# Stick-breaking attention: order of the score blocks and value products between two head pairs

## The reference, cut to what matters

```python
z = einsum('bhtd,bhsd->bhts', q, k) / sqrt(64)
log_1mb = where(s < t, log_sigmoid(-z), 0)
suffix = cumsum(log_1mb, axis=3, reverse=True) - log_1mb
a = exp(where(s < t, log_sigmoid(z) + suffix, -inf))
out = einsum('bhts,bhsd->bhtd', a, v)
```

## Time and profile before

| | |
|---|---|
| median of 3 runs | 1989.14 us (1988.02 to 1990.04) |
| span of the profiled execution | 1987.1 us |
| its own time with what lies around the span | not given |
| PE busy | 1948.0 us, 98% |
| DVE busy | 1116.1 us, 56% |
| ACT busy | 859.2 us, 43% |
| mean granted clock of PE | 0.997 |
| stage of the attention pairs | about 1031 to 1234 us of the span |

### The profile page before, as it was taken

How to read it: one execution, slowest core, us unless ns; L and a number is a source line. 1 busy time by engine, 2 the same in 40 slices (tenths; PEclk the granted TensorE clock), 3 DMA queues, 4 the chain that set the end, 5 groups by cost and what they waited for, 6 DMA issues and landing times.

```text
span 1987.1 us, 25948 instructions
## 1 busy us (share of the span) xinstructions
PE 1948.0 (98%) x10434; PEld 1588.1 (80%) x10434; DVE 1116.1 (56%) x1824; ACT 859.2 (43%) x1528; POOL 89.6 (5%) x109
## 2 busy tenths in 40 slices
PE   8999999999999999999999999999999999999997
PEld 6688877888888888888877778888898788888886
DVE  5677745644465444423648888884645465444323
ACT  4355642533343222222447777774435453222221
POOL 0100000000020000000200000011200020000000
PEclk9999999999999999999999999999999999999999
DMA  7111121333323333333322222113243223333331
GB/s 278 61 54 43 54 70 59 90 96 93 104 75 96 95 96 92 92 88 91 94 75 58 63 64 63 45 55 105 64 132 103 85 77 94 95 96 93 87 98 62
DMA packets 49432, 170.56 MB, mean 86 GB/s; under 512 B 5520, under 2 KB 8080, under 8 KB 48928
## 3 DMA queue, kind: packets, MB, share of 16 engines
q1 hardware_dynamic: 48816, 166.73, 27.9%
q0 software_dynamic: 496, 2.16, 0.3%
HBM read 166.77 MB, written 2.10 MB: 85 GB/s over the span
## 4 chain that ended last, share of the span: by engine, by line
PE 91%; DVE 6%; ACT 2%; issue 1%; DMA 0%; SPq 0%; DVEq 0%
PE acc L1852 56%; PE bank L1852 18%; PE acc L2006 2%; PE bank L1941 2%; PE bank L2188 1%; PE acc L2388 1%; PE bank L1978 1%; PE bank L2223 1%; PE bank L2126 1%; DVE bank L1216 1%; DVE w_lo L1136 1%; PE bank L2375 1%; PE bank L2409 1%; DVE residual L1222 1%; PE bank L1874 1%
## 5 line engine op out<-in xcount | busy, mean ns | idle before, releaser
L1136 DVE TENSOR_TENSOR w_lo<-w_raw,w_hi 128x1024 fp32r<-128x1024 f32 (+2 forms) x306 | 365.7, 1198 | 330.5 <-ACT w_hi L602 330.1
L1852 PE MATMUL acc<-act_hi,w_hi 128*128 128x512 f32 (+1 forms) x1096 | 431.0, 393 | 17.4 <-DVE w_lo L1136 9.6
L1852 PE MATMUL acc<-act_lo,w_hi 128*128 128x512 f32 (+1 forms) x1096 | 419.3, 383 | 0.0
L1852 PE MATMUL acc<-act_hi,w_lo 128*128 128x512 f32 (+1 forms) x1096 | 419.3, 383 | 0.0
L602 ACT ACTIVATE w_hi<-w_raw 128x1024 fp32r<-128x1024 f32 (+2 forms) x306 | 314.3, 1028 | 210.9 <-PE acc L1852 181.0
L1852 PEld LDWEIGHTS acc<-act_hi,w_hi 128*128 128x128 f32 x1096 | 206.4, 188 | 68.4 <-issue 16.1
L1852 PEld LDWEIGHTS acc<-act_hi,w_lo 128*128 128x128 f32 x1096 | 206.4, 188 | 44.1
L1852 PEld LDWEIGHTS acc<-act_lo,w_hi 128*128 128x128 f32 x1096 | 206.6, 188 | 43.2 <-issue 2.2
L1852 PE MATMUL bank<-act_hi,w_hi 128*128 128x512 f32 (+1 forms) x520 | 192.6, 370 | 1.2 <-DVE w_lo L1136 1.2
L1852 PE MATMUL bank<-act_lo,w_hi 128*128 128x512 f32 (+1 forms) x520 | 191.0, 367 | 0.0
L1852 PE MATMUL bank<-act_hi,w_lo 128*128 128x512 f32 (+1 forms) x520 | 190.9, 367 | 0.0
(11 more groups left out here) (457 smaller groups left out, 3182.7 us busy)
## 6 DMA issues: line engine op xcount, KB each, us to landing
w_raw<-w_all SPq DMA_DIRECT2D x282, 512.0 KB, 3.5
w_raw<-w_all SPq DMA_DIRECT2D x16, 384.0 KB, 3.3
residual<-xT SPq DMA_DIRECT2D x8, 256.0 KB, 7.7
cmp_w_k<-w1k SPq DMA_DIRECT2D x1, 2048.0 KB, 8.6
cmp_w_v<-w1v SPq DMA_DIRECT2D x1, 2048.0 KB, 12.7
w_raw<-w_all SPq DMA_DIRECT2D x8, 256.0 KB, 2.7
out_t<-residual SPq DMA_DIRECT2D x16, 128.0 KB, 1.7
ret_decay<-decay POOLq DMA_DIRECT2D x4, 256.0 KB, 3.3
```

The lines of the kernel that those rows point to most:

```text
L1136: TT(WL[:, c % RAW_RING, 0:nb * P], WR[:, c % RAW_RING, 0:nb * P], WH[:, c % HI_RING, 0:nb * P].bitcast(F32), ALU.subtract).then_inc(s_lo, 1)
L1852: ins = MM(bank[:, cols], w[:, at, k * P:(k + 1) * P], x, start=first and r == 0 and k == 0, stop=last and r == 2 and k == nb - 1)
```

## The change

The next pair's scores become one run, in the order of blocks 0, 1, first half of 4, first part of 3, first part of 2, second part of 3, second half of 4, second part of 2. It stands in front of all the values of the pair, behind all five copies of the transposed weights. The first two steps (6 matmuls) of the turn's first gemm are put ahead of the run, the other six follow the values. Two semaphores count the scores, one for blocks 0, first half of 4 and 2, the other for 1, 3 and second half of 4; ACT's Abs waits for these. In the last pair, which has no next one, the values too now wait for all copies. DVE's program is unchanged.

```diff
+BEFORE_SCORES = 2
...
             def sb_abs(p, b):
-                act.wait_ge(sem("sb_scored"), p * 5 + b + 1)
+                if b in (1, 3):
+                    act.wait_ge(sem("sb_scored_second"), 3 * p + (1 if b == 1 else 2))
+                else:
+                    act.wait_ge(sem("sb_scored_first"), 3 * p + {0: 1, 4: 2, 2: 3}[b])
+                if b == 4:
+                    act.wait_ge(sem("sb_scored_second"), 3 * p + 3)
...
+            def scores(p):
+
+                first, second = sem("sb_scored_first"), sem("sb_scored_second")
+                scored(0, parts_of(0), p).then_inc(first, 1)
+                scored(1, parts_of(1), p).then_inc(second, 1)
+                scored(4, parts_of(4)[0:1], p).then_inc(first, 1)
+                scored(3, parts_of(3)[0:1], p)
+                scored(2, parts_of(2)[0:1], p)
+                scored(3, parts_of(3)[1:2], p).then_inc(second, 1)
+                pe.wait_ge(first, 3 * p + 2)
+                scored(4, parts_of(4)[1:2], p).then_inc(second, 1)
+                scored(2, parts_of(2)[1:2], p).then_inc(first, 1)
...
-            long_blocks(0)
-            middle_blocks(0)
-            last_block(0, True)
+            scores(0)
             v_turn(0)
-            last_block(0, False)
             mixed(MIX_FIRST[1:])
             for p in range(SB_PAIRS):
...
+                if more:
+                    gemm("sb_mix", MIX_AT[MIX_TURNS[p][0]], HH, HL, ks=range(BEFORE_SCORES))
                 pe.wait_ge(sem("sb_early_t"), p * 2 + 2)
+                pe.wait_ge(sem("sb_late_t"), p * 3 + 3)
                 if more:
                     qkv_ready(p + 1, "qk")
-                    long_blocks(p + 1)
+                    scores(p + 1)
                 pe.wait_ge(sem("sb_v_tokens"), p + 1)
                 values(3, (0, 1))
-                pe.wait_ge(sem("sb_late_t"), p * 3 + 2)
-                if more:
-                    middle_blocks(p + 1)
                 values(2, (2, 3))
                 values(0, (2, 3))
-                pe.wait_ge(sem("sb_late_t"), p * 3 + 3)
-                if more:
-                    last_block(p + 1, True)
                 values(1, (4,)).then_inc(sem("sb_pv"), 1)
                 if more:
-                    last_block(p + 1, False)
-                    mixed(MIX_TURNS[p][0:2])
+                    gemm("sb_mix", MIX_AT[MIX_TURNS[p][0]], HH, HL, ks=range(BEFORE_SCORES, DK))
+                    mixed(MIX_TURNS[p][1:2])
                     qkv_ready(p + 1, "v")
```

## The result

The change takes 2031.68 us (median of 4 runs, 2031.38 to 2032.58) against 1989.02 for the kernel before in the same session: ratio 1.0218, 95% interval 1.0205 to 1.023. The profiled execution has a span of 2030.1, 43.0 longer than before. Here is the head of its page: PE has the same 10434 matmuls and 5.7 us more of busy time, so the loss is waiting and slower work, not more of it.

A forecast was written before the change was run, and what follows sets the result against it. PE, busy 98% of the span, was taken as the bound by its own work. Waits and pair changes of +29.7 plus clock falls of 11.9 gave +41.6 on 1989.1, forecast 2030.7 us, range 2017 to 2042.

The forecast's parts named there:

- The low part at the filler: PE waits before the two early gemm steps for DVE's low part of the weights, T + 2.18 to 8.06: 5.9 idle.
- Rival 1: Low part is there in time at the filler: a pair takes 24.41, total 1980.5 us; chance 0.06.
- The single runs and the waits: On PE, scores in one run take 2.34, values 2.33; waits for late copies and block 4 add nothing within pairs.
- The 2.13: Time of the new score run without its ends: 1280 columns on each head, two passes at 2.4 GHz.
- rival 3: Unequal score blocks don't overlap on two heads: 2.56 instead of 1.28 in each of 8 runs, +10.2, 2041; chance 0.10.
- The clock: PE's clock falls to half after each of seven new idles, 1.7 each, 11.9 together; bounds for one 0 and 3.4.
- rival 2: Stalls come without clock falls: 1989.1 + 29.7 = 2018.8 us; chance 0.14.
- Unequal blocks: Score blocks of unequal length on two heads were taken to overlap fully in the new run, 1.28 instead of 2.56.
- the 10 us that the prediction drew from the rule: If matmuls keep program order, six score blocks behind 0 and 1 could run serially, up to 10 us longer in sum.
- The chain of logs: ACT and DVE prepare the next weights by T + 29.3, needed at 32.0: 2.7 to spare, so no bound.
- Rival 4: The chain of logs becomes the bound behind the stall: 0.7 to 1 more a pair, 2036 us; chance 0.06.
- The ends: First pair's scores save 0.7; last pair's values wait for the last DVE copy, +0.7.

The follow-up runs named there:

- kept-busy kernel: The change plus 24 useless 128x512 matmuls (11 in pair 0) into idle bank PS[5] before each filler: 2016.70 us, ratio 1.0144 to the kernel before.
- third experiment: Mended kernel, but the accumulator of turn[1] emptied behind the late copies as before, only the low part early: 1993.76 us, ratio 1.0027 to the kernel before.
- mended kernel: The change plus, on DVE, turn[1]'s accumulator emptied and the filler's low part made before the late copies: 1978.56 us, ratio 0.9952 to the kernel before.
- the one with equal neighbours: Mended kernel with the run of scores in the old order, block 4's halves one behind the other: 1983.80 us, ratio 0.9977 to the kernel before.

## Why the prediction was right

The forecast was 2030.7, the result 2031.68.

- *The low part at the filler.* Right in place and size: filler forecast at T + 8.06, found at 8.07; DVE's low part at T + 8.01 as before. Shown by taking it away: without filler, or with the DVE work moved, the loss is gone. Rival 1 is out for the change as it was made, and its mechanism is right: where the low part and the accumulator are there in time, the pair takes 24.30 (forecast 24.41).
- *The single runs and the waits.* At full clock runs of 2.36 and 2.34, forecast as 2.34 and 2.33. The 2.13 is right in size, but not as it was worked out: 1280 columns in two passes at one column a cycle of 2.4 GHz would be 1.07. The row has 0.62 less 0.19 for its ends, 0.43, for the two passes of 256 columns, and five times that is the 2.13; the 2.56 of rival 3 is counted in the same way. The kept-busy kernel shows the sum of the pair at full clock to the hundredth, 30.29. I didn't name the wait for the accumulator as the next one; the third experiment found it, 3.9 us before the wait for the low part ends. That wait changes nothing of the forecast for this kernel.
- *The clock.* A fall at each of seven stalls, as forecast; rival 2 is out (14.1 between the change and the kept-busy kernel). The term was sized too low: 7 x 1.7 = 11.9 against 13.9 in the trace. I took the row of one fall of 3.41; here six of seven stretches lasted 6.83, of which 3.4 or 5.5 fell into work, so a stall cost 1.5 or 2.6. The span grew by 43.0 against 41.6: +2.0 from this term and +1.3 from before the first changed instruction, -1.5 from a fall elsewhere that went away and -0.3 from the ends. That the last three nearly cancel is luck.
- *Unequal blocks.* Overlapped, as taken; rival 3 is out: a run of unequal blocks takes 2.36, and serial blocks behind 0 and 1 would have made it 3.6. The Trainium skill (TensorE: Matmul & The Clock Gate, Part 3: Packing small matmuls) has matmuls start in program order. The trace agrees: in the mended kernel's run in pair 2, the first passes of the six blocks behind 0 and 1 start at 1104.99, 1105.00, 1105.42, 1105.64, 1105.87 and 1106.07 with 256, 384, 384, 128, 256 and 128 columns, the order of the program. They overlap in that order, so the 10 us that the prediction drew from the rule didn't follow from it.
- *The chain of logs.* Not the bound, as said: the kept-busy pairs of 30.29 are PE's own sum, and even pairs of 24.30 don't wait for it. Rival 4 is out.
- *The ends.* First scores -0.8 (forecast -0.7), last pair +0.45 (forecast +0.7): before, PE had also waited a little for the last exponential there.

## What to carry to other kernels

Work put in front as a filler has operands of its own: before moving a block of a gemm ahead, look up in the trace when each thing it waits for is made, its weights' last preparation and its free accumulator, for it holds up the whole queue behind it. When a filler waits, don't drop it before looking whether the engine that feeds it was idle just before; here two steps moved forward on DVE turned +2.2% into -0.5%. And an idle of several us on PE costs more than its length, because the work behind it starts at half clock.

## What the runs showed of the hardware that I had not expected

- The low clock after a stall of 5.7 lasts 6.83, not 3.41 as after the shorter idles, and begins 2.3 to 4.7 us after the idle does. Idles of 2.83 and 5.72 brought a fall seven times out of seven, idles of 1.79 once in seven, idles of 1.15 to 1.20, seven of them, never. The idle of 1.6 behind the pairs is the same in all nine traces and was followed by a fall in three of them, those of the kernel before, of the mended kernel and of the one with equal neighbours.
- PE starts score blocks of 512, 384, 256 and 128 columns on two halves of its rows so closely that the run is 0.2 longer than the columns of one half. Running the two halves of block 4, one on each head but both in one bank, behind each other at the run's end costs 0.74 a run, more than the 0.43 of one half's columns; how the other 0.3 comes about wasn't told apart.
